# The first 64 tokens of an expert layer go by gathered rows instead of the dense products

## What is computed

```python
def peer(h, w_query, keys_1, keys_2, expert_u, expert_v):
    ...
        q = (hc @ w_query).reshape(PEER_CHUNK, PEER_HEADS, PEER_KEY_DIM)
        s1 = jnp.einsum('chk,nk->chn', q[..., :PEER_HALF_DIM], keys_1)
        s2 = jnp.einsum('chk,nk->chn', q[..., PEER_HALF_DIM:], keys_2)
        ...
        top_s, pos = lax.top_k(cand, PEER_TOPK)
        experts = jnp.take_along_axis(cand_idx, pos, axis=-1)
        gate = jax.nn.softmax(top_s.astype(jnp.float32), axis=-1).astype(hc.dtype)
        u = jnp.take(expert_u, experts, axis=0)
        act = jax.nn.gelu(jnp.einsum('chkd,cd->chk', u, hc))
        v = jnp.take(expert_v, experts, axis=0)
        return jnp.einsum('chk,chkd->cd', gate * act, v)
```

## Time and profile before

| | |
|---|---|
| time, median of 3 runs | 3052.13 us (3051.16 to 3052.43) |
| the profiled execution | 3052.59 us, span in the trace 3050.8 us |
| TensorE matmul busy | 2993.0 us, 98% of the span |
| DVE, ACT, POOL busy | 1570.8, 1148.5, 1763.6 us |
| moved by DMA | 482 MB, 158 GB/s on average |

### The profile page before, as it was taken

The page is one execution under the profiler, slowest core; times in us unless marked ns, Lnnn a source line. Parts: engine busy times, 40 slices in busy tenths (PEclk is TensorE's granted clock), DMA queues, the critical chain, the costliest instruction groups (busy, mean ns, idle before and its releaser), DMA issues.

```text
span 3050.8 us, 43979 instructions
## 1 busy us (share of the span) xinstructions
PE 2993.0 (98%) x14710; PEld 2439.5 (80%) x14710; DVE 1570.8 (51%) x2729; ACT 1148.5 (38%) x1507; POOL 1763.6 (58%) x2020
## 2 busy tenths in 40 slices
PE   7899999999999999999999999999999999999998
PEld 5777888877788887887888888888888888888887
DVE  7957555234355532995229975444312554444443
ACT  5554222246432223333333335555543333323332
POOL 2635776644367764975546765444445666656663
PEclk9999999999999999999999999999999999999999
DMA  8316555422145552222224445555565656555652
GB/s 333 110 36 228 193 192 175 134 83 70 56 159 193 186 168 88 98 83 83 97 87 144 138 151 180 206 201 202 202 230 182 206 171 213 203 186 170 211 203 72
DMA packets 170318, 482.25 MB, mean 158 GB/s; under 512 B 15360, under 2 KB 48896, under 8 KB 168192
## 3 DMA queue, kind: packets, MB, share of 16 engines
q1 hardware_dynamic: 147680, 410.83, 40.2%
q10 hardware_dynamic: 22560, 70.37, 5.9%
HBM read 411.93 MB, written 69.21 MB: 158 GB/s over the span
## 4 chain that ended last, share of the span: by engine, by line
PE 62%; POOL 20%; issue 15%; DVE 2%; ACT 1%; DMA 0%; POOLq 0%; ACTq 0%; DVEq 0%
PE ps L1883 59%; POOL w_lo L580 20%; PE pa L1883 3%; DVE ada L1199 0%; DMA cols<-in_cols 0%; DVE s_tmp L1731 0%; DVE mg_lo L1733 0%; DVE h_lo L1287 0%; ACT mg_hi L1047 0%; DVE s_m L1729 0%; DVE x L1252 0%; ACT w_hi L601 0%; DVE sq L1281 0%; DVE w_lo L1315 0%; POOLq L578 0%
## 5 line engine op out<-in xcount | busy, mean ns | idle before, releaser
L580 POOL TENSOR_TENSOR w_lo<-raw,w_hi 128x256 fp32r<-128x256 f32 x2016 | 1763.4, 907 | 1258.7 <-ACT w_hi L601 1257.8
L1883 PE MATMUL ps<-h_hi,w_hi 128*128 128x512 f32 x2392 | 944.1, 395 | 13.1 <-ACT h_hi L693 7.0
L1883 PE MATMUL ps<-h_hi,w_lo 128*128 128x512 f32 x2392 | 935.4, 391 | 0.0
L1883 PE MATMUL ps<-h_lo,w_hi 128*128 128x512 f32 x2392 | 912.3, 390 | 0.0
L601 ACT ACTIVATE w_hi<-raw 128x1024 fp32r<-128x1024 f32 x509 | 538.9, 1060 | 822.9 <-PE ps L1883 682.2
L1883 PEld LDWEIGHTS ps<-h_hi,w_hi 128*128 128x128 f32 x2392 | 451.2, 189 | 112.6 <-issue 11.0
L1883 PEld LDWEIGHTS ps<-h_hi,w_lo 128*128 128x128 f32 x2392 | 451.2, 189 | 93.7 <-issue 0.2
L1883 PEld LDWEIGHTS ps<-h_lo,w_hi 128*128 128x128 f32 x2392 | 449.8, 188 | 91.9 <-issue 0.7
L1883 PE MATMUL ps<-wa_hi,w_hi 128*128 128x512 f32 x1024 | 398.8, 389 | 0.0
L1883 PE MATMUL ps<-wa_hi,w_lo 128*128 128x512 f32 x1024 | 398.8, 389 | 0.0
L1883 PE MATMUL ps<-wa_lo,w_hi 128*128 128x512 f32 x1024 | 398.7, 389 | 0.0
(11 more groups left out here) (350 smaller groups left out, 2902.9 us busy)
## 6 DMA issues: line engine op xcount, KB each, us to landing
ada<-in_ada SPq DMA_DIRECT2D x144, 512.0 KB, 4.6
raw<-in_expert_u SPq DMA_DIRECT2D x128, 512.0 KB, 3.7
raw<-in_expert_v SPq DMA_DIRECT2D x128, 512.0 KB, 4.0
raw<-in_ffn_in SPq DMA_DIRECT2D x88, 512.0 KB, 3.6
expert_act<-g_act ACTq DMA_DIRECT2D x128, 256.0 KB, 3.4
gate_matrix<-w_st ACTq DMA_DIRECT2D x16, 2048.0 KB, 6.5
e_w<-gate_matrix SPq DMA_DIRECT2D x16, 2048.0 KB, 11.0
e_g<-expert_act SPq DMA_DIRECT2D x128, 256.0 KB, 7.6
```

Of the source, the lines that this page charges most:

```text
L580: last = nc.gpsimd.tensor_tensor(w_lo[:, k, c:c + 256], raw[:, k, c:c + 256], w_hi[:, k, c:c + 256].bitcast(F32), ALU.subtract)
L1883: return nc.tensor.matmul(out, a, b, start=start, stop=stop_)
```

## The change

1. `GT` = 64 tokens leave the dense expert products. Their products, gelu, gates and additions are 448 columns wide (`ND`), the tiles in the arena move, and some semaphores are used a second time. The gate matrix has 14 pieces of 32 tokens instead of 16, and `U_FIRST`, `U_GATES` go from 48, 64 to 56, 56.
2. For these 64 tokens the rows are gathered. The 64 tokens lie on the partitions twice, and each partition takes 64 of the 128 picks of its token. POOL issues 64 indirect transfers from `expert_u` and 64 from `expert_v`, each of 128 rows of 4 KB. DVE does a product and sum of each `u` row with the token (`dve_dot`), ACT one gelu over all, and DVE adds each `v` row, scaled, into one of two sums in PSUM (`dve_row`). At the end two sums are added, and 8 small products bring them to the layout of `x`.
3. The places: POOL's program is written out from `expert_u` block 56 on, with at most one gather behind a block's four subtractions. A `u` gather uses 3 buffers, a `v` gather 4, and each waits until DVE has used the row that lay in its buffer (`row_used`). `dots_by` and `rows_by` say how many are due by a block, for POOL and for DVE.
4. The double norm is halved too: the squares are scaled by a root of the squared gain plus epsilon (`roots`), so that one sum gives both norms. The table for Ln and Exp is asked for one tile earlier in every norm, and in the attention's output an addition goes ahead of `dve_mod`.

```diff
+GT = 64
+ND = S - GT
+PKS = P // GT
+ROWS = P // PKS
+U_SLOTS, V_SLOTS = 3, 4
-U_FIRST, U_GATES = 48, 64
+U_FIRST, U_GATES = 56, 56
...
+    U_BLOCKS = U_GATES + U_LAST
+    V_FROM, V_DOTS = 26, 32
+    def dots_by(b):
+        if b < U_GATES:
+            return max(0, b) * 3 // 4
+        if b < U_BLOCKS:
+            return U_GATES * 3 // 4 + (b - U_GATES) // 4
+        return min(ROWS, U_GATES * 3 // 4 + U_LAST // 4 + (b - U_BLOCKS) * 5 // 8)
+    def rows_by(v):
+        return min(ROWS, max(0, v - V_DOTS) * 3 // 4)
...
+        def gather_v():
+            j = issued["v"]
+            issued["v"] += 1
+            if j >= V_SLOTS:
+                pool.wait_ge(row_used, ROWS + j - V_SLOTS + 1)
+            nc.gpsimd.indirect_dma_start(out=t_out[j % V_SLOTS][:, :], out_offset=None, in_=v_rows,
+                                         in_offset=bass.IndirectOffsetOnAxis(ap=t_ix[:, j:j + 1], axis=0))\
+              .then_inc(v_in[j % V_SLOTS], 16)
+        for m in range(gates // RING * RING, last):
             split(m, m % RING)
+            b = m - gates
+            if b == 1:
+                pool.wait_ge(row_ready, 2)
+                pool.wait_ge(rt_mm, 1)
+                for _ in range(U_SLOTS):
+                    gather_u()
+            if b >= 2 and issued["u"] < min(ROWS, U_SLOTS + dots_by(b - 1)):
+                gather_u()
+            v = m - M0["expert_v"]
+            if v >= V_FROM and issued["v"] < min(ROWS, V_SLOTS + rows_by(v)):
+                gather_v()
...
-            nc.scalar.activation(rstd[:, :], pa[:, 0, :], ACT.Copy, scale=EPS).then_inc(eps_done, 1)
-            act.wait_ge(both_done, 1)
-            own_a.link(act, nc.scalar.activation(gsum[:, :], gsum[:, :], ACT.Ln, scale=1.0 / D, bias=EPS * EPS))
-            nc.scalar.activation(gsum[:, :], gsum[:, :], ACT.Exp, scale=-0.5).then_inc(rs_ready, 1)
...
+    def act_roots(act):
+        own_a.link(act, nc.scalar.activation(roots[:, :], cols[:, COLS[PLAIN[4]]:COLS[PLAIN[4]] + DT], ACT.Square))
+        own_a.link(act, nc.scalar.activation(roots[:, :], roots[:, :], ACT.Ln, bias=EPS))
+        nc.scalar.activation(roots[:, :], roots[:, :], ACT.Exp, scale=0.5).then_inc(roots_done, 1)
...
+    def dve_dot(dve, j):
+        row = t_row[j % U_SLOTS]
+        dve.wait_ge(u_in[j % U_SLOTS], 16 * (j // U_SLOTS + 1))
+        nc.vector.tensor_tensor_reduce(out=row[:, :], in0=row[:, :], in1=t_h[:, :], scale=1.0, scalar=0.0,
+                                       op0=ALU.mult, op1=ALU.add, accum_out=t_dot[:, j:j + 1]).then_inc(row_used, 1)
+    def dve_row(dve, j):
+        a = 2 * (j % 2)
+        total = pa[:, a:a + 2, :]
+        dve.wait_ge(v_in[j % V_SLOTS], 16 * (j // V_SLOTS + 1))
+        if j >= 2:
+            dve.wait_ge(row_used, ROWS + j - 1)
+        nc.vector.scalar_tensor_tensor(out=total, in0=t_out[j % V_SLOTS][:, :].rearrange("p (b n) -> p b n", b=2),
+                                       scalar=t_act[:, j:j + 1], in1=total, op0=ALU.mult, op1=ALU.add).then_inc(row_used, 1)
...
+        for g in range(NG - 1):
+            for k in range(GE):
+                gated(g + 1, k, (g + 1) % 2)
+                add(g, k)
+                n = GE * g + k
+                for j in range(dots_by(U_BLOCKS + n), dots_by(U_BLOCKS + n + 1)):
+                    dve_dot(dve, j)
...
+                for j in range(rows_by(n), rows_by(n + 1)):
+                    dve_row(dve, j)
...
+        group(NG - 2)
+        pe.wait_ge(row_ready, 3)
+        for k in range(DT):
+            last = mm(pa[:, 0, k * GT:(k + 1) * GT], t_sum[:, k * P:(k + 1) * P], t_sel[:, :], True, True)
+        last.then_inc(row_mm, 1)
+        group(NG - 1)
```

More of the change, by code:

```diff
@@ L1149, in act_peer @@
                     wa_part(g + 1, k, (g + 1) % 2, i)
+        with act.Fori(0, V_DOTS // (2 * GE)) as i:
+            two_groups(i)
+        act.wait_ge(row_used, ROWS)
+        nc.scalar.activation(t_act[:, :], t_dot[:, :], ACT.Gelu_apprx_tanh).then_inc(row_copied, 1)
+        with act.Fori(V_DOTS // (2 * GE), NG // 2 - 1) as i:
+            two_groups(i)
         hi.skip(GE * (NG - 2))
@@ L1266, in dve_norm, with dve_add @@
             dve_lo(dve, n, k)
-    def dve_add(bank, gate, k, norm):
+    def dve_add(bank, gate, k, norm, first=0):
+        TA = slice(first, S // 2)
         if k == DT - 1 and norm in HALVED:
@@ L1275, in dve_add @@
             return
-        nc.vector.scalar_tensor_tensor(out=x[:, k, :], in0=bank, scalar=gate, in1=x[:, k, :],
+        nc.vector.scalar_tensor_tensor(out=x[:, k, first:], in0=bank[:, first:], scalar=gate, in1=x[:, k, first:],
                                        op0=ALU.mult, op1=ALU.add).then_inc(tile_free, 1)
@@ L1768, in dve_router @@
         dve.wait_ge(rs_out, 4 * TT)
+        for a in range(PKS):
+            last = v.tensor_tensor(t_dup[:, :, a * GT:(a + 1) * GT], h_hi[:, :, 0:GT].bitcast(F32),
+                                   h_lo[:, :, 0:GT].bitcast(F32), ALU.add)
+        last.then_inc(row_ready, 1)
         with dve.Fori(0, TT) as i:
@@ L1797, in dve_router @@
         v.tensor_tensor(e, e, bc(z1, 2, TK), ALU.mult).then_inc(gate_done, 1)
+        dve.wait_ge(gate_done, 1)
+        for a in range(PKS):
+            rows, picks = slice(a * GT, (a + 1) * GT), slice(a * ROWS, (a + 1) * ROWS)
+            v.scalar_tensor_tensor(out=t_dot[rows, :], in0=r_i[0:GT, 0, 0, picks], scalar=float(NK), in1=r_i[0:GT, 1, 0, picks],
+                                   op0=ALU.mult, op1=ALU.add)
+            last = v.tensor_copy(t_gate[rows, :], r_i[0:GT, 2, 0, picks])
+        step(last)
+        v.tensor_copy(t_ix[:, :], t_dot[:, :]).then_inc(row_ready, 1)
+        v.tensor_tensor(t_sel[:, :], ident[:, 0:GT], ident[:, GT:2 * GT], ALU.add)
         v.tensor_copy(iota_t[:, :, :], bc(iota, 2, 2))
@@ L2304, in first @@
             for d in range(DT):
-                last = unit(out, (m + k) % RING, d * P, h_hi[:, d, :], h_lo[:, d, :], d == 0, d == DT - 1)
+                last = unit(out[:, GT:], (m + k) % RING, d * P, h_hi[:, d, GT:], h_lo[:, d, GT:], d == 0, d == DT - 1)
             last.then_inc(blk_done, 1)
@@ L2311, in pe_peer @@
                 first(m, T, k, i, RING)
+        pe.wait_ge(row_ready, 1)
+        for d in range(DT):
+            last = nc.tensor.transpose(pa[:, d // 4, d % 4 * P:(d % 4 + 1) * P], t_dup[:, d, :], ident)
+        last.then_inc(row_mm, 1)
         for k in range(U_FIRST - RING, U_FIRST - RING // 2):
```

240 lines of the change are left out of this document (134 added, 106 removed).

## The result

The changed kernel takes 3063.55 us (median of 9 runs), the kernel before 3053.21 beside it: 1.0036 times as long, 95% interval 1.0025 to 1.0047; its runs spread from 3052.65 to 3073.87 us, those of the kernel before from 3051.16 to 3060.93. Forecast was 3002 us, 1.7% faster. It is slower by a third of a per cent: inside the range, on the other side of no change.

The account below looks back on a forecast made before the run. The prediction took TensorE's work to bound the expert blocks; 89 us gained in the first product, 45 lost in the second and 5.5 gained in the norms took the span from 3050.8 to 3001, so 3002 us, range 2935 to 3065.

Parts of the forecast that it names:

- The norms: Double norm between last addition and first expert product: halving it and asking earlier for the table gains 5.5 us.
- The first product: Expert `u` part: narrower products and eight gate blocks made plain, less added transposes, gain 89 us.
- Both fit: Gate stage: POOL and DVE can take three quarters of a gather and of a dot in each 5.82 us block.
- The gather's cost: POOL time of one gather of 128 rows: taken as 1.5 us, between bounds of 0.38 and 3.44 us.
- X: The assumed POOL time of one gather, 1.5 us; each further us was to cost 42 us in all.
- What the wait adds: Second expert product: gather waits tie POOL to the block just ended; 2.4 us lost every two blocks, 9.6 a group.
- DVE's own chain: Second expert product: `e_w` load, rows and additions make DVE 2.9 us late a group, mostly hidden; 0.5 us added.
- The dearer level of `e_t`: DVE's `e_t` in the expert layer: 1.27 us instead of 0.67; 30 us in sum if every block paid it.
- The clock: Second expert product: slow first products behind some of the longer TensorE gaps cost 4 us in all.
- The distance of the products: Both expert products: 448-column products stand 200 ns apart, 4.80 us a block of 24.
- the gather is dear: Rival: a gather takes POOL longer, break-even at 2.7 us, 3083 us total at 3.44; chance 0.18.
- the wait doesn't bite: Rival: gathers run early enough, leaving only DVE's chain (nine groups x 1) and the first group: 2905 us; chance 0.06.

Follow-up runs that it names:

- width_only: The changed kernel without the gathers, dots and row products, its narrow products alone: 2907.5 us, ratio 0.952 against the kernel before.
- lead3: The changed kernel with each gather of the second expert product issued three blocks later in POOL's program: 2958.8 us, ratio 0.970 against the kernel before.
- split_ew: The changed kernel with the load of `e_w` cut in halves, each loaded once its four experts are used: 3039.0 us, ratio 0.9955 against the kernel before.
- fill: `split_ew` with five useless products on TensorE ahead of the `w_lo` wait, every second block of groups 4 to 13: 3011.6 us, 0.987 of the kernel before.
- quarter_wait: `split_ew` with an extra 256-column POOL pass behind each of 60 gathers of the second expert product: 3093.8 us, ratio 1.0147 against the kernel before.
- lead_split: The changed kernel with second-product gathers three blocks later and the `e_w` load in halves: 2914.6 us, 0.9545 of the kernel before; 2918.5 us when run again.
- after: The changed kernel itself, as profiled, against the kernel before: 3063.55 us, ratio 1.0036.

## Why the prediction was wrong

The step that failed is a term of the sum for the second product, the slow clock behind gaps: put at 4 us, it measured 43. Step by step, against the sum -89 + 45 - 5.5:

- **The norms**: 5.9 us gained (the first expert product starts at 1574.37, before at 1580.23), 5.5 predicted. Right.
- **The first product**: from 1574.37 to 2258.9 are 684.5 us, where it took 763: 78 gained, 89 predicted. The gate blocks took 5.84 us, as forecast (5.82); POOL waited there for a dot now and then, and TensorE never for POOL. The 11 us are 7 for the distance of the products (0.203 for 0.200) and one gap of 3.3 behind an `oh_gate` on DVE, the one that took 6.44 us. "Both fit" held for DVE with some luck: 2.6 us a block and three quarters of a dot would be 3.5 to 4.0, and DVE was busy 332 of 347 us there, 5.6 a block, since 27 of its instructions took 3.7 us and more (`width_only`: 172 of 343).
- **The gather's cost**: 1.11 us, not 1.5, inside the bounds and nearer to SP's issue than I took it. The rule that I had set beside it (the Trainium skill, page DMA: Bandwidth & Descriptors, section Latency and other measured facts: about 1 us to the first byte) is near this row, though the row shows how long POOL was busy and not the first byte. By the prediction's price of 42 us for each us, X = 1.1 should have brought 17 us (the prediction has these 17 for X = 1, where its own price gives 21); the next point ate it.
- **What the wait adds**: the mechanism was right in its place, its rhythm and nearly its size. Gaps come at every second block from 35 on; the turn was forecast as 7.2 us, counted from the first product of the next block, and so counted it took 7.2 at block 53 (2577.72 to 2584.94): the shorter gather against handovers of 0.4 for 0.16 and longer subtractions (3.65 for 3.44). At the 34 gaps that aren't named in the next point it took 6.1 to 7.6, mostly less than forecast. All gaps of the second product were forecast as 742 - 614 - 4 = 124 us, and are 126; that it comes so close is luck, since the next point stands against this one.
- **DVE's own chain**: I let it "mostly vanish" under the other. In the changed kernel it makes the first gap of six groups 4.3 to 5.2 us instead of 2; in the sum of the gaps this stands against the cheaper gather. `lead3` left it alone on the path (42 us of gaps, the first group and the end included), `split_ew` took it away. Group 4, for which I had 10.5 us, took 53.6 where its work is 38.9; 7.1 us of this are the gap at block 32, and the `wa_lo` of 8.53 us stands in front of it. The dearer level of `e_t` (30 us if every block paid it) didn't come: its median is 0.62 us.
- **The clock: this term failed.** "Some of the longer gaps will cost that, 4": it was 43 us. `fill` shows that the standing causes it: with the gaps filled in part, the slow products fell from 33 us to some 9 though `w_lo` came no sooner.
- **The distance of the products** in the second product: 625 us for 614, the other part of the 448 columns' 3 ns.

Together: 39 (clock) + 11 (second product) + 7 + 3 (first) + 2 (gaps) - 0.4 = 62 us, and the result is 61.6 above the forecast.

The clock could have been read. Behind the earlier trace rows I looked at the first product only, 0.76 us for 0.47, and priced a gap by it. The rows right behind it, in the kernel before, were these:

```profile
1213.90 0.63 PE L1883 MATMUL ps<-h_hi,w_lo 128*128 128x512 f32 x1
...
1215.61 0.63 PE L1883 MATMUL ps<-h_hi,w_lo 128*128 128x512 f32 x1
1216.03 0.47 PE L1883 MATMUL ps<-h_hi,w_hi 128*128 128x512 f32 x1
1216.34 0.39 PE L1883 MATMUL ps<-h_hi,w_lo 128*128 128x512 f32 x1
```

Seven products took 3.00 us from 1213.34, where 7 x 0.2267 = 1.59: 1.4 us for one gap of 3 us. Times the 40 gaps that I forecast, that is 56 us as an estimate, and the forecast would have been about 3055, "no change"; most gaps were shorter than these 3 us, and only 19 of the 40 had a slow stretch, so that it comes near is in part luck. The Trainium skill, page TensorE: Matmul & The Clock Gate, section HAM oscillation — how this bites in real kernels, tells of the same cost in a kernel whose bursts of products are shorter than its waits: it pays for the return to the full clock in each burst. Here the bursts are longer than the waits (two blocks, 9.8 us, against 2), and the cost came all the same, if not in every burst: clock 0.93 over the second product.

Of the rivals, "the gather is dear" ended on the right side, for a reason that isn't there (the gather is cheap). The break-even which I gave for X belonged to a sum without the clock; `quarter_wait`, on `split_ew`, gives the slope with it: 1.17 us more cost 55 us, 47 us for each, where I had 42. And "the wait doesn't bite", with DVE's chain left in, is what `lead3` built: 2905 forecast (its own terms add up to 2910), 2958.8 measured, because that chain costs far more than 1 us a group. Only `lead_split`, without the chain, comes near it: 2914.6.

Left open: which gaps are followed by one slow product and which by eleven. Of two gaps with 2.0 us of idle time, one (block 45) had eleven in the block behind it and the other (block 61) one, so the length of the gap alone doesn't decide it. Why the distance has two values at widths between 384 and 512 wasn't tried, nor what brings DVE's long instructions.

## What to carry to other kernels

A buffer's release puts a wait on the engine that refills it, and whatever stands behind the refill waits too: issue the refill late enough in that engine's program that its wait is always met (here one block later, in two lines of code: 2914.7 us against 3039.0, both with the halved load), and only then ask what it costs. When a forecast has TensorE standing again and again, price each gap as the gap plus the slow products behind it, read from several rows after a gap in the trace. A load into a single buffer that starts only when the last reader is done is harmless as long as the reader has slack: with shorter blocks alone it still was (`width_only`, 2907.5 us). It became the bound when DVE got the dots and rows as well (`lead3`, 2958.8); split it by what is free first. And when an engine gets new work, look at what the durations of its neighbours' instructions do, not only at the sum of busy times.

## What the runs showed of the hardware

- Gathers of 128 rows of 4 KB by index on POOL took 0.94 to 1.80 us of the engine, 1.11 in the mean of the 64 from `expert_v` and 1.15 of all, and 128 of them hid behind TensorE almost wholly (`lead_split` against `width_only`: 7 us).
- Gaps of about 2 us were followed by up to 11 slow products (1.2 GHz), which cost 1.7 us; longer ones (4.3 to 5.2 us) by 8 to 16, up to 2.9 us. Behind a shorter gap the clock could fall after TensorE had started again (block 53: 1.1 to 1.4 us after). Useless products in the gap brought 27 us.
- DVE instructions with two inputs in SBUF took 3.7 to 8.5 us, for 0.6 to 1.9 otherwise, until a run of 4 to 12 POOL subtractions behind a gather was done (`after`: 27 in the gate stage; none over 1.8 us in `width_only`).
- The distance of products isn't straight in their width: 0.1734, 0.1900, 0.2027, 0.2178 and 0.2267 us for 384 to 512 columns in steps of 32. At 416, 448 and 480 columns it has a second value: 0.1867, 0.2067 and 0.2200 us.
